# The upper page of an expert's down weights, loaded in two halves, and a down pass that takes all lower rows first

## The chip, the core and the metric

The kernel runs on one of the eight cores of a Trainium2 chip. A core has TensorE (PE) for matmuls, VectorE (DVE) and ScalarE (ACT) for elementwise work and for emptying PSUM, GpSimd (POOL), and SyncE (SP), which here issues nearly all loads. All loads of SP go through one queue (q1), served by the core's 16 DMA engines. The metric is the device time of one execution in microseconds.

## What is computed

One layer on 256 tokens of width 1024: a mixer (chunked attention and spatial gating, merged by gates) and then a mixture of experts, in which each token goes to 4 of 32 experts. The second part is the one that matters here:

```python
h = rmsnorm(x, g_pre_ffn) * (1 + sc2) + sh2
logits = h @ w_router + b_router                 # top 4 of 32 per token, softmax over the four
for e in experts:                                # x_e: the tokens that chose e
    gu = x_e @ w_gate_up[e] + b_gate_up[e]       # 1024 x 2048 f32, 8 MB
    act = min(gu[:, :1024], 7) * sigmoid(1.702 * min(gu[:, :1024], 7)) * (clip(gu[:, 1024:], -7, 7) + 1)
    y_e = act @ w_down[e] + b_down[e]            # 1024 x 1024 f32, 4 MB
out = x + gt2 * rmsnorm(sum of gate * y_e over the chosen experts)
```

All weights are float32. The 32 experts together have 384 MB of them, and each is read once.

## The kernel before

The mixer takes the first part of the span, and its pages of weights pass through a ring of five places. From about 270 us on, the experts run one after the other, each on a list of the tokens that chose it. The list is cut into blocks of 64 tokens, the last of which is narrow (32 tokens) where it is short enough. A 64-token block runs as matmuls of 64 columns of stationary data by 512 moving ones (rows with 128*64), a narrow one as 32 by 256 (rows with 128*32), four to a step k instead of two. There are 37 blocks: 27 experts have one, five have two.

A block on PE is, in order: the gather of its tokens (L1418), the bias (L1427), transposes (L1433), the gate-up pass over k = 0..7 (L1454), `combine` of the block before (L1399), transposes of the activations (L1440) and of the combine table (L1467), and the down pass over eight k (L1483), which ends with `s_y`. The down pass multiplies rows k of `w_down`: k = 0..3 stand in the lower page `dlo_w`, k = 4..7 in the upper page `dhi_w`.

**Where the weights stand.** An expert has six pages of 2 MB: four of gate-up (`gu_w`, two slots, so that experts take turns), the lower down page (`dlo_w`, two slots), and the upper down page `dhi_w`, of which there is one place only (page 10 of the arena). The next expert's upper page can thus be loaded only once the last block of the expert before has finished its down pass.

**What sets the order of the loads.** SP works through a list written out by hand (L443 to L461). In the turn in which expert j is computed it does: wait until the last block's gate-up pass has used the first page (`s_gfree`), load gate-up page 0 of expert j+2; wait for the second page, load page 1; wait until all blocks of expert j are done (`s_y`), load the upper page of expert j+1; and then, behind that wait and without one of their own, the bias, gate-up pages 2 and 3 and the lower page of expert j+2. After the loop it waits for `s_y` of expert 30 and loads the upper page of expert 31, followed by the residual `x1_back` (1 MB) and `gain2` (0.5 MB). The queue thus serves, per expert, gate-up 0 and 1 (j+2), upper page (j+1), gate-up 2, 3 and lower page (j+2).

**What sets the order of the down pass.** `order` sorts the k so that those come first whose activations are turned first (`s_aTev`, `halves[0]`); k in the second half wait for `halves[1]`. In a narrow block (q = 2) that gives 0, 2, 4, 6, 1, 3, 5, 7, in a 64-token block (q = 4) 0, 1, 4, 5, 2, 3, 6, 7. The wait for the upper page (`s_dhi`) stands at k = 4, thus third in both.

## Time and profile before

| | us |
|---|---|
| median of 3 runs | 1217.56 (1217.47 to 1218.21) |
| the profiled execution, its own time | 1217.57 |
| its span, first to last instruction | 1215.3 |
| PE busy in the span | 1037.6 (85%) |
| PE weight loads | 515.7 (42%) |
| DVE busy | 282.4 (23%) |
| ACT busy | 189.9 (16%) |
| POOL busy | 30.8 (3%) |
| moved by DMA | 464.91 MB, mean 383 GB/s |
| mean granted TensorE clock | 0.943 of full |

The profiled execution lies on the median, and 2.3 us of its time lie outside the span. PE is the busiest engine, but its share is an average over stretches with different limits, so the line of GB/s over 40 slices of 30.4 us each must be read beside it.

### The profile page before, as it was taken

The numbers are of one execution on the slowest core, as the hardware profiler recorded it, in microseconds if no ns is written. First come the engines' busy times: TensorE is split into PE (matmuls) and PEld (weight loads), VectorE is DVE, ScalarE is ACT, GpSimd is POOL, SyncE is SP. The second block draws the span as 40 slices with busy tenths as digits, with TensorE's granted clock in tenths as the row PEclk, the third lists the DMA queues.
The fourth block names the chain that finished last, engine by engine and source line by source line (L and its number), as shares of the span: only waits on it lengthen the run. The fifth ranks groups of instructions, "written<-read, shape, count | busy, mean of one in ns | idle before, by whom it ended". The sixth has DMA issues, their size and how long they took to land.

```text
span 1215.3 us, 21516 instructions
## 1 busy us (share of the span) xinstructions
PE 1037.6 (85%) x8327; PEld 515.7 (42%) x8329; DVE 282.4 (23%) x793; ACT 189.9 (16%) x458; POOL 30.8 (3%) x54
## 2 busy tenths in 40 slices
PE   3899999977786999988988898889898989696966
PEld 2756887643343334324433433343334333233333
DVE  5433554152121111211121112111211121111112
ACT  2112443031010111101111111111111111010102
POOL 1000100130000000000000000000000000000000
PEclk9899999987797999989998999899999999898988
DMA  9979650989999969999999999999999999999996
GB/s 357 390 280 331 256 218 12 422 328 387 425 424 425 427 244 424 425 425 406 426 426 424 404 426 427 425 391 427 426 422 402 428 423 426 427 424 425 425 426 266
DMA packets 59948, 464.91 MB, mean 383 GB/s; under 512 B 5380, under 2 KB 7500, under 8 KB 27032
## 3 DMA queue, kind: packets, MB, share of 16 engines
q1 hardware_dynamic: 59184, 462.47, 92.4%
q0 software_dynamic: 336, 1.07, 0.3%
q10 hardware_dynamic: 408, 1.10, 0.2%
q8 instruction: 14, 0.23, 0.1%
q14 instruction: 6, 0.05, 0.0%
HBM read 462.50 MB, written 2.11 MB: 382 GB/s over the span
## 4 chain that ended last, share of the span: by engine, by line
PE 56%; DMA 36%; DVE 3%; issue 3%; ACT 1%; DVEq 0%; SPq 0%; POOL 0%; ACTq 0%
DMA arena<-in_w_down_dram 34%; PE pp L1454 15%; PE pp L1483 15%; PE pp L1245 5%; PE pp L1178 4%; PE pp L1418 2%; PE pp L1258 2%; PE po L1315 2%; PE pp L1188 2%; PE po L1399 2%; DMA arena<-in_w_ada_dram 2%; PE pp L1427 1%; PE pp L1433 1%; DVE h_sb L788 1%; ACT work L702 1%
## 5 line engine op out<-in xcount | busy, mean ns | idle before, releaser
L1454 PE MATMUL pp<-arena,work 128*32 128x256 f32 (+1 forms) x3840 | 374.6, 446 | 20.1 <-ACT work L702 20.1
L1483 PE MATMUL pp<-arena,work 128*32 128x256 f32 (+1 forms) x1920 | 208.7, 485 | 78.8 <-DMA arena<-in_w_down_dram 78.8
L1454 PEld LDWEIGHTS pp<-arena,work 128*32 128x32 f32 (+1 forms) x3840 | 167.5, 117 | 210.9 <-issue 126.7
L1483 PEld LDWEIGHTS pp<-arena,work 128*32 128x32 f32 (+1 forms) x1920 | 81.6, 130 | 187.0 <-DMA arena<-in_w_down_dram 90.6
L1021 DVE TENSOR_SCALAR work<-pp 128x128 f32<-128x128 f32 (+1 forms) x74 | 25.0, 338 | 403.2 <-PE pp L1454 403.2
L705 ACT ACTIVATE work<-work 128x128 f32<-128x128 f32 (+1 forms) x74 | 25.9, 350 | 403.5 <-DVE work L1021 403.5
L1418 PE MATMUL pp<-h_sb,work 128*32 128x256 f32 (+1 forms) x480 | 60.5, 465 | 33.1 <-issue 28.6
L1015 DVE COPY work<-pp 128x256 f32<-128x256 f32 (+1 forms) x37 | 19.4, 525 | 264.1 <-PE pp L1418 264.1
L1399 PE MATMUL po<-work 64*128 64x512 f32 x304 | 75.5, 615 | 1.2 <-ACT work L721 1.2
L1245 PE MATMUL pp<-arena 128*128 128x256 f32 x256 | 59.1, 390 | 0.0
L788 DVE SCALAR_TENSOR_TENSOR h_sb<-arena,small,h_sb 128x1024 f32<-128x1024 f32 x42 | 53.9, 1284 | 7.1 <-DMA arena<-in_w_ada_dram 5.9
L1245 PEld LDWEIGHTS pp<-arena 128*128 128x128 f32 x256 | 49.1, 194 | 8.9 <-issue 2.2
L1418 PEld LDWEIGHTS pp<-h_sb,work 128*32 128x32 f32 (+1 forms) x480 | 21.6, 121 | 71.3 <-issue 64.0
L1399 PEld LDWEIGHTS po<-work 64*128 64x128 f32 x304 | 26.1, 186 | 41.0 <-issue 39.3
L1178 PE MATMUL pp<-arena 128*128 128x256 f32 x192 | 43.3, 387 | 0.0
L1178 PEld LDWEIGHTS pp<-arena 128*128 128x128 f32 x192 | 37.5, 196 | 6.7 <-issue 1.5
L1033 DVE TENSOR_SCALAR work<-iota,rank 128x64 f32 x74 | 15.4, 251 | 96.3 <-issue 91.3
L1037 DVE TENSOR_SCALAR work<-iota,rank,gate_tab 128x64 f32 x148 | 36.2, 308 | 0.0
L719 ACT COPY work<-pp 128x256 f32<-128x256 f32 x23 | 8.6, 372 | 169.0 <-PE pp L1483 169.0
L702 ACT COPY work<-pp 128x256 f32<-128x256 f32 (+1 forms) x37 | 16.8, 453 | 106.3 <-PE pp L1433 106.3
L1427 PE MATMUL pp<-bgu,pick 4*32 4x256 f32 (+1 forms) x480 | 32.2, 470 | 0.0
L1258 PE MATMUL pp<-arena 128*128 128x256 f32 x128 | 28.4, 380 | 0.0
(219 smaller groups left out, 642.0 us busy)
## 6 DMA issues: line engine op xcount, KB each, us to landing
arena<-in_w_gate_up_dram SPq DMA_DIRECT2D x128, 2048.0 KB, 27.4
arena<-in_w_down_dram SPq DMA_DIRECT2D x64, 2048.0 KB, 24.3
arena<-in_w_ada_dram SPq DMA_DIRECT2D x11, 2048.0 KB, 7.7
arena<-in_w_in_dram SPq DMA_DIRECT2D x5, 2048.0 KB, 16.8
arena<-in_w_gate_dram SPq DMA_DIRECT2D x4, 2048.0 KB, 12.7
arena<-in_w_out_dram SPq DMA_DIRECT2D x2, 2048.0 KB, 10.7
arena<-in_w_ada_dram SPq DMA_DIRECT2D x2, 1024.0 KB, 23.4
arena<-in_w_branch_a_dram SPq DMA_DIRECT2D x1, 2048.0 KB, 7.5
```

The costliest lines, as they stand in the source:

```text
L702: a.copy(hgT[:, 0:w], pp[:, TURN, 0:w]).then_inc(s_turned, 1)
L705: a.activation(sig[:, hh, 0:w // 2], glu[:, hh, 0:w // 2], ACT.Sigmoid, scale=ALPHA).then_inc(s_sig, 1)
L788: ins = v.scalar_tensor_tensor(out=acc[:, n % 2, :], in0=page_k(pg, k), scalar=c_act[:, kk:kk + 1], in1=acc[:, n % 2, :], op0=ALU.mult, op ...
L1037: ins = v.tensor_scalar(selg[:, t, c, :], places, rank[:, t, e], gate_tab[:, t, e], ALU.is_equal, ALU.mult)
L1178: mm = t_.matmul(ps[:, i * TOK:(i + 1) * TOK], page_k(pg, k)[:, m * P:(m + 1) * P], hT[:, k, :], start=(k == 0), stop=(k == KD - 1))
L1245: mm = t_.matmul(ps[:, i * TOK:(i + 1) * TOK], page_k(pg, k)[:, m * P:(m + 1) * P], hT[:, k, :], start=(k == 0), stop=(k == KD - 1))
L1258: mm = t_.matmul(branch_bank(m)[:, half * TOK:(half + 1) * TOK], page_k(page_of(name), k)[:, m * P:(m + 1) * P], src[:, k, :], start=(k == 0),
L1399: mm = t_.matmul(po[:, 2 * t + j, :], selgT[j * TB:(j + 1) * TB, t, :], y_sb[j * TB:(j + 1) * TB, :], start=False, stop=last, skip_group_c ...
L1418: mm = t_.matmul(pp[j * m:(j + 1) * m, TOKS, 0:w], sel[:, t, 0:m], h_sb[:, t, j * w:(j + 1) * w], start=(t == 0), stop=(t == TT - 1))
L1427: t_.matmul(pp[j * m:(j + 1) * m, UP[hh], 0:w].rearrange("p (s f) -> p s f", s=2), pick[rows, r, 0:m], bgu[rows, :, cols], start=True, sto ...
L1454: mm = t_.matmul(pp[j * m:(j + 1) * m, UP[hh], 0:w].rearrange("p (s f) -> p s f", s=2), hgT[:, at:at + m], gu_w[slot][:, k, :, r * PAIR:(r ...
L1483: mm = t_.matmul(pp[j * m:(j + 1) * m, UP[0], 0:w], actT[:, at:at + m], wd[:, j * w:(j + 1) * w], start=(n == 0), stop=(n == KD - 1))
```

## The change

The upper page is loaded by two DMAs of 1 MB, one for k = 4 and 5 and one for k = 6 and 7, each with its own semaphore. PE waits for the first at k = 4 and for the second at k = 6. The down pass takes the k in the order 0, 2, 1, 3, 4, 5, 6, 7 in a narrow block and 0 to 7 in a 64-token block, so the wait for the second half of the activations moves from the fifth to the third step. The matmul that ends the sixth step signals `s_dhi_free`, and on this signal SP loads the first half of the next upper page. The second half, and all that stands behind it, still waits for `s_y`.

```diff
-            def load_dhi(e):
-                sp.dma_start(dhi_w.rearrange("p (g r) d -> p g (r d)", r=2), dn_v[e, :, 2:4, :]).then_inc(s_dhi, 16)
+            def load_dhi(e, r):
+                sp.dma_start(dhi_w[:, 2 * r:2 * r + 2, :].rearrange("p k d -> p (k d)"),
+                             dn_v[e, :, 2 + r, :]).then_inc(s_dhi[r], 16)
...
-            load_dhi(0)
+            for r in range(2):
+                load_dhi(0, r)
...
+                    sp.wait_ge(s_dhi_free, total)
+                    load_dhi(last_e, 0)
                     sp.wait_ge(s_y, total)
-                    load_dhi(last_e)
+                    load_dhi(last_e, 1)
...
-            sp.wait_ge(s_y, sp.snap(done, min_val=1, max_val=NEXP * NBLK))
-            load_dhi(sp.snap(dhi_expert, min_val=0, max_val=NEXP - 1))
+            total = sp.snap(done, min_val=1, max_val=NEXP * NBLK)
+            last_e = sp.snap(dhi_expert, min_val=0, max_val=NEXP - 1)
+            sp.wait_ge(s_dhi_free, total)
+            load_dhi(last_e, 0)
+            sp.wait_ge(s_y, total)
+            load_dhi(last_e, 1)
...
-                order = sorted(range(KD), key=lambda k: (k % q >= q // 2, k))
+                order = sorted(range(KD), key=lambda k: (k >= 4, k >= 6, k % q >= q // 2, k))
                 for n, k in enumerate(order):
-                    if k == 4:
-                        pe.wait_ge(s_dhi, dhi_landed)
-                    if n == KD // 2:
+                    if k in (4, 6):
+                        pe.wait_ge(s_dhi[k // 2 - 2], dhi_landed)
+                    if n == 2:
                         pe.wait_ge(s_aTev, halves[1])
...
+                    if n == 5:
+                        mm.then_inc(s_dhi_free, 1)
```

How it moves instructions is seen at two places. First PE's queue in the down pass of a narrow block of the first slot (the matmul is L1483 before and L1492 now; `s_dlo0` is the lower page, `s_dhi` the upper one, `s_aTev` the turned activations). Before:

```order
L1483 MATMUL pp<-arena,work 32x256 [waits s_dlo0]
L1483 MATMUL pp<-arena,work 32x256 x7
L1475 ISA
L1483 MATMUL pp<-arena,work 32x256 [waits s_dhi]
L1483 MATMUL pp<-arena,work 32x256 x7
L1483 MATMUL pp<-arena,work 32x256 [waits s_aTev]
L1483 MATMUL pp<-arena,work 32x256 x11
L1483 MATMUL pp<-arena,work 32x256 [waits s_selTev]
L1483 MATMUL pp<-arena,work 32x256 x3
```

Now:

```order
L1492 MATMUL pp<-arena,work 32x256 [waits s_dlo0]
L1492 MATMUL pp<-arena,work 32x256 x7
L1492 MATMUL pp<-arena,work 32x256 [waits s_aTev]
L1492 MATMUL pp<-arena,work 32x256 x7
L1484 ISA
L1492 MATMUL pp<-arena,work 32x256 [waits s_dhi0]
L1492 MATMUL pp<-arena,work 32x256 x7
L1492 MATMUL pp<-arena,work 32x256 [waits s_dhi1]
L1492 MATMUL pp<-arena,work 32x256 x3
L1492 MATMUL pp<-arena,work 32x256 [waits s_selTev]
L1492 MATMUL pp<-arena,work 32x256 x3
```

Of the 32 matmuls 24 stood behind the wait for the upper page; now 16 stand behind the first half's wait, and 8 of these behind the second half's. (The profile counts each of these f32 matmuls twice, so a narrow down pass is x64 in its rows and one k is x8.)

Second, SP's queue in one turn of the loop (L372 and L373 load gate-up, L402 and L403 the upper page, L398 and L399 the lower page). Before:

```order
L372 DMA arena<-in_w_gate_up_dram 128x4096 [waits s_gfree]
L402 ISA [waits s_y]
L402 DMA arena<-in_w_down_dram 128x2x2048
L454 ISA
L369 DMA bgu<-in_b_gate_up_dram 4x2x256 x2
L372 ISA
L372 DMA arena<-in_w_gate_up_dram 128x4096
```

Now:

```order
L373 DMA arena<-in_w_gate_up_dram 128x4096 [waits s_gfree]
L403 ISA [waits s_dhi_free]
L403 DMA arena<-in_w_down_dram 128x2048
L403 ISA [waits s_y]
L403 DMA arena<-in_w_down_dram 128x2048
L459 ISA
L370 DMA bgu<-in_b_gate_up_dram 4x2x256 x2
L373 ISA
L373 DMA arena<-in_w_gate_up_dram 128x4096
```

One load of half the size has moved ahead of the wait for `s_y`, and everything behind the upper page stands where it stood.

## Rows read from the trace of the kernel before

**Rows 1.** The page's second part: GB/s moved in each of 40 slices.

```profile
GB/s 357 390 280 331 256 218 12 422 328 387 425 424 425 427 244 424 425 425 406 426 426 424 404 426 427 425 391 427 426 422 402 428 423 426 427 424 425 425 426 266
```

**Rows 2.** Waits: engine, line, releaser, us in total, times, longest.

```profile
PE pp L1483 <- DMA arena<-in_w_down_dram: 78.8, 18, 10.2
```

**Rows 3.** Timeline of PE, 1061 to 1126: start, us, engine, line, work, [idle before].

```profile
1061.79 5.35 PE L1483 MATMUL pp<-arena,work 128*32 128x256 f32 x48 [10.19 <-DMA arena<-in_w_down_dram]
...
1091.53 5.37 PE L1483 MATMUL pp<-arena,work 128*64 128x512 f32 x24 [0.64 <-DMA arena<-in_w_down_dram]
...
1121.39 4.86 PE L1483 MATMUL pp<-arena,work 128*32 128x256 f32 x48 [10.13 <-DMA arena<-in_w_down_dram]
```

**Rows 4.** By stretch: PE, PEld, DVE, ACT, POOL busy; granted clock, DMA share, GB/s.

```profile
520.93:640.83 119.90, 106.16 (x975) 45.37 (x975) 21.61 (x75) 14.74 (x41) 0.00 (x0) 0.97 1.00 420
640.83:762.00 121.17, 105.99 (x974) 45.26 (x974) 21.61 (x75) 14.74 (x41) 0.00 (x0) 0.98 1.00 420
762.00:882.15 120.15, 107.04 (x974) 45.49 (x974) 21.60 (x75) 14.75 (x41) 0.00 (x0) 0.97 1.00 417
882.15:1002.18 120.03, 107.75 (x975) 45.35 (x975) 21.59 (x75) 14.74 (x41) 0.00 (x0) 0.97 1.00 419
1002.18:1181.15 178.97, 139.74 (x1104) 56.16 (x1105) 26.72 (x90) 17.77 (x48) 0.00 (x0) 0.90 1.01 425
```

**Rows 5.** Timeline of PE, 288 to 450: first expert's down pass, then the long hole.

```profile
288.36 3.66 PE L1483 MATMUL pp<-arena,work 128*32 128x256 f32 x64
...
390.02 5.32 PE L1483 MATMUL pp<-arena,work 128*32 128x256 f32 x48 [10.17 <-DMA arena<-in_w_down_dram]
...
417.16 1.94 PE L1483 MATMUL pp<-arena,work 128*64 128x512 f32 x8
419.56 5.37 PE L1483 MATMUL pp<-arena,work 128*64 128x512 f32 x24 [0.46 <-DMA arena<-in_w_down_dram]
...
446.19 7.09 PE L1483 MATMUL pp<-arena,work 128*64 128x512 f32 x32
```

**Rows 6.** Timeline of SP, loads only: first turns and the long hole.

```profile
292.23 0.38 SPq L402 DMA_DIRECT2D arena<-in_w_down_dram  x1
...
433.56 3.10 SPq L372 DMA_DIRECT2D arena<-in_w_gate_up_dram  x2
453.47 0.38 SPq L402 DMA_DIRECT2D arena<-in_w_down_dram  x1
```

**Rows 7.** Busy time by stretch at three holes, columns as in rows 4.

```profile
291.00:296.00 5.00, 1.02 (x20) 0.37 (x12) 1.31 (x6) 1.10 (x3) 0.00 (x0) 1.00 0.85 288
...
444.00:458.00 14.00, 13.39 (x114) 5.26 (x114) 3.12 (x11) 2.40 (x6) 0.00 (x0) 1.00 0.33 118
...
692.00:698.00 6.00, 3.96 (x72) 1.81 (x64) 0.94 (x4) 1.47 (x4) 0.00 (x0) 1.00 0.85 318
```

**Rows 8.** Timeline of PE, 670 to 693: a two-block expert.

```profile
670.86 5.37 PE L1483 MATMUL pp<-arena,work 128*64 128x512 f32 x24 [1.29 <-DMA arena<-in_w_down_dram]
...
689.45 3.66 PE L1483 MATMUL pp<-arena,work 128*32 128x256 f32 x64
```

**Rows 9.** Timeline of all engines, 1181 to 1207: the end.

```profile
1181.15 5.35 PE L1483 MATMUL pp<-arena,work 128*32 128x256 f32 x48 [10.00 <-DMA arena<-in_w_down_dram]
...
1186.73 0.38 SPq L402 DMA_DIRECT2D arena<-in_w_down_dram  x1
...
1200.28 3.66 PE L1483 MATMUL pp<-arena,work 128*32 128x256 f32 x64
...
1206.46 0.69 DVE L1083 TENSOR_TENSOR arena<-po,gain 128x512 f32<-128x512 f32 x1 [7.28 <-PE po L1399]
```

**Rows 10.** DMA issues of SP after 1186.5: us from issue to landing last.

```profile
arena<-in_w_down_dram SPq DMA_DIRECT2D x1, 2048.0 KB, 14.2
...
gain<-gain_dram SPq DMA_DIRECT2D x1, 512.0 KB, 17.0
```

**Rows 11.** Busy time by stretch around the last long wait, columns as in rows 4.

```profile
1181.15:1186.50 5.35, 5.35 (x52) 2.33 (x56) 0.00 (x0) 0.00 (x0) 0.00 (x0) 0.50 1.01 432
```

More of the change, by code:

```diff
@@ L278, in block_program @@
         s_dlo = [sem(f"s_dlo{b}") for b in range(2)]
-        s_dhi = sem("s_dhi")
+        s_dhi = [sem(f"s_dhi{r}") for r in range(2)]
+        s_dhi_free = sem("s_dhi_free")
         s_nblk, s_selg = sem("s_nblk"), sem("s_selg")
```

## The prediction

> **What bounds the kernel now.** I read the line of GB/s first [rows 1]. From the eleventh slice on it stands at 422 to 428 nearly everywhere, the highest the kernel reaches: the expert part is bound by the load queue. What deviates is lost time: one slice at 244, a few between 391 and 406, and the last at 266. Then the waits: PE waits 18 times for a down page in the down pass, 78.8 us in all [rows 2]. That looks like the thing to gain, but it is not: while the queue runs at 425, PE's wait is only the other side of a full queue. The timeline shows it. Upper pages land at 1061.79, 1091.53 and 1121.39 [rows 3], and six in a row take 178.97 us, or 29.83 us each, at 425 GB/s [rows 4]. Nothing that PE does sooner makes such a stretch shorter. Time can come only from three places: holes in the queue, the tail behind the last landing, and the cost of a load.
>
> A hole arises since there is one place for the upper page. SP loads it after `s_y`, and all that follows queues behind that wait. Behind a landed upper page some 22 us of other pages are queued. An expert with one block is through in time; one with two is not, and the queue runs dry.
>
> **Prices.** One k of the down pass is 3.66 / 8 = 0.46 us in a narrow block [rows 5], and 5.35 / 6 = 0.89 us after a long wait [rows 3], where the granted clock is 0.50, that is 1.2 GHz [rows 11]. In a 64-token block it is 7.09 / 8 = 0.89 us [rows 5]. Half an upper page is 1.05 MB, 2.47 us at 425 GB/s, so the first half lands 2.5 us before the second. In the long hole the stretch 444 to 458 moved 14 x 118 kB/us = 1.65 MB [rows 7], 3.9 us at full rate, of which about 1.2 stood ahead of the hole; so data flowed again near 455.3, 1.8 us after the issue at 453.47 [rows 6].
>
> **Step 1, the first hole.** The first expert's down pass ends at 292.02 [rows 5], the load follows at 292.23 [rows 6] into a queue that is drying (288 GB/s from 291 to 296 [rows 7]: 5 x 137 / 425 = 1.6 us lost). Its first half will be issued two narrow k earlier, 0.9 us. The half covers 2.5 us, so that the second, issued after `s_y`, follows without a gap. Gain 0.9, and everything in the queue up to the next hole comes 0.9 earlier.
>
> **Step 2, the long hole,** behind the one expert with two 64-token blocks. Its chain starts at the landing at 390.02: six k, 5.32 us, to 395.34 [rows 5]. Now four k are done before the page, two before its second half, and only k = 6 and 7 follow the landing: 1.8 us, 3.6 earlier, 4.5 with step 1. The next block reaches its down pass at 412.7 instead of 417.16 [rows 5], and does four k by 416.3. Its halves land at 419.56 - 0.9 - 2.5 = 416.2 and 418.7; k = 6 and 7 end at 420.4 instead of 424.93. The second block has no wait and ends at 448.8 instead of 453.28; its sixth step at 447.0. The load comes at 447.2 instead of 453.47, 6.3 us earlier. The two gate-up loads of 433.56 [rows 6] move by 4.5 as well, so the small hole in front of them closes. Against it: more matmuls may run at 1.2 GHz, since the block that follows starts 3.6 us sooner after the landing; before, the clock rose at about the end of the down pass (at 1121.39 the 48 matmuls took 4.86 instead of 5.35 [rows 3], so their last part was already fast). The 64-token gather and bias behind it could lose up to 2 us. I take 0.5 and have 5.8 for steps 1 and 2 together, bounds 4.3 and 6.3.
>
> **Step 3, the holes behind the four experts of one 64-token and one narrow block.** Example: the page lands at 670.86; three quarters of a down pass, 5.37 us; the narrow block ends at 693.11 [rows 8]; the hole is seen as 318 GB/s from 692 to 698 [rows 7]. Now `s_dhi_free` comes 1.8 + (693.11 - 676.23) - 0.9 = 17.8 us after the landing, and data 1.8 us later, at 19.6, while the queue lasted 22. So the hole closes with some 2.4 us to spare, which also covers the 2 us that the clock may cost. What the holes are worth, in two ways. By rate: the four stretches run at 420, 420, 417 and 419 instead of 425 [rows 4], which is 1.4 + 1.4 + 2.3 + 1.7 = 6.8 us. By landings: 16 experts took 481.25 us [rows 4], at 29.83 each they would take 477.3, so 4.0. I take the middle, 5.4.
>
> **Step 4, the tail.** The last upper page is issued at 1186.73 [rows 9] and lands 14.2 us later [rows 10], at 1200.9, 19.8 us after the one before (1181.15). The last block comes to its down pass at 1200.28, so it hardly waits, and ends at 1203.94 [rows 9]. Now the block starts 3.6 earlier, is at its down pass at 1196.7 (1198.2 if the clock costs 1.5), is through k = 0 to 5 by about the landing, and ends 0.9 us behind it, at 1201.9 on the old scale: 2.0 earlier. But `gain2`, last in the queue, lands 17.0 us after its issue near 1187.7 [rows 10], at 1204.7, and DVE wants it at 1206.46 - 2.0 = 1204.5 [rows 9]: what comes next is late by 0.2. I take 1.7, bounds 0.5 and 1.8.
>
> **Step 5, what is added.** There are 31 more loads in the loop. In the dense stretch an expert has eight loads (two of them tiny) at 425; if the difference to the best slice (428 [rows 1]) is laid on them, they cost 0.2 us per expert, 0.026 each, 0.8 for 31. I take 0.4, bounds 0 and 0.8. The added wait on PE is for data that was awaited anyway. The wait for the activations' second half moves two k forward; its copy is done before the down pass starts in narrow blocks and two k (1.8 us) remain in 64-token ones: nothing. SP's added wait holds back only the second half's wait, which ends later anyway.
>
> **Sum.** 5.8 + 5.4 + 1.7 - 0.4 = 12.5 us. The profiled execution took 1217.57, 0.01 from the median; 1205.1. With all bounds at their bad ends 4.3 + 4.0 + 0.5 - 0.8 = 8.0, so 1209.6; at their good ends 6.3 + 6.8 + 1.8 = 14.9, so 1202.7.
>
> **Rivals.**
> *The queue pays for each load (ends slower).* Halves may cost the queue something that two-megabyte loads hide. The dearest row is the restart: 1.8 us from issue to data. Shown in full by 31 halves that would be 56 us: 1261. It turns the sign at (12.5 + 2.4) / 31 = 0.48 us per half, and gives no change between 0.33 and 0.48. Against it: loads follow each other at 425 GB/s with the starts hidden [rows 4], and the contiguous piece per partition stays 8 KB. For it: no 1 MB load stands in the dense part. Slower 0.06, no change 0.05.
> The Trainium skill, "DMA: Bandwidth & Descriptors", section "Bandwidth", speaks against the change: it measures 6.15 us for 1 MB (341 GB/s) against 425 GB/s for 16 MB, with a fixed part of about 2.0 us per DMA. By that fixed part the sum would be 62 us dearer, 1267; the trace disagrees for loads that queue, since 2 MB loads run at 425 in rows 4.
>
> *The halves land together,* if the engines work on both at once. Then only the order counts: four k follow each landing instead of six. Steps 1 and 2 give 0.9 + 1.8 + 1.8 = 4.5, step 3 still 4.0, the tail 0.9, less 0.4: 9.0, so 1208.6. Chance 0.08.
>
> *The clock takes it back.* PE has more work at 1.2 GHz behind every long wait; with all bounds bad and 1 us more in the tail, 1210.6. For it: the fall to 0.50 [rows 11] is there. Against it: the queue, not PE, ends the dense stretches. Chance 0.10.
>
> *The small holes stay,* if 417 to 420 has another cause than `s_y`. Without step 3: 1210.5. Chance 0.05.
>
> **How the numbers follow.** My forecast has 0.64 and lies from 1202.7 to 1208; another 0.02 lies below. The range 1201.5 to 1212 holds these and the three mild rivals. A measurement of this kernel tells 0.2%, 2.4 us, from no change. Faster by more: 0.64 + 0.02 + 0.08 + 0.10 + 0.05 = 0.89; within: 0.05; slower: 0.06.
>
> **What would show it.** Slices from the eleventh on at 424 or more, but for one of about 300 where 244 stood; the restart behind the long hole 6 us earlier; two waits in the down passes, the second at most 0.8 us; 29.8 us from landing to landing; the first half 2.5 us ahead. Dense stretches below 423 GB/s would prove the first rival, and small holes left behind the two-block experts the last.

## The result, and the profile after

| | median us | runs | ratio to the kernel before, 95% |
|---|---|---|---|
| before | 1218.16 | 1217.47 to 1218.69 | |
| changed kernel | 1211.37 | 1209.77 to 1215.44 | 0.9948 (0.9928 to 0.9967) |
| predicted | 1205.1 | 1201.5 to 1212.0 | |

The change saves 6.8 us, where 12.5 were forecast. The sign was right and the time lies inside the range, near its upper end, but the gain came out at about half. The runs also differ more among themselves: those of the changed kernel lie within 5.7 us, and within 4.0 when it was run again; those of the kernel before lie within 1.2 here and, in the larger sets of 9 to 15 runs beside the experiments, within 2.1 to 4.7. The profiled execution is the slowest of the five (1215.44, span 1213.2), so it shows what can go wrong better than what mostly happens; the same kernel profiled again (run `again`, below) had a span of 1209.6.

The page of the profiled execution, GB/s in 40 slices of 30.3 us, answering [rows 1]:

```profile
GB/s 358 385 263 333 256 240 11 421 332 362 424 425 426 425 293 422 424 424 425 427 426 423 382 428 426 425 364 424 425 425 424 425 424 425 426 426 425 426 426 279
```

The slice of the long hole rose from 244 to 293. Of the four slices with small holes (406, 404, 391, 402) the first and the last are closed (425, 425), but the two in the middle are worse than before: 382 and 364. The slice of the first hole (the tenth) is worse as well: 362 instead of 387. Waits for down pages in the down pass are down from 78.8 us to 58.7 [rows 2], now in two parts each:

```profile
PE pp L1492 <- DMA arena<-in_w_down_dram: 58.7, 21, 9.5
```

By stretch, cut at landings of the upper page's second half, answering [rows 4] (PE, PEld, DVE, ACT, POOL busy, granted clock, DMA share, GB/s):

```profile
519.20:638.35 119.15, 106.07 (x975) 44.55 (x975) 21.62 (x75) 14.73 (x41) 0.00 (x0) 0.98 1.01 425
638.35:761.41 123.06, 110.79 (x974) 45.63 (x974) 21.62 (x75) 14.73 (x41) 0.00 (x0) 0.93 1.00 415
761.41:883.26 121.85, 110.30 (x974) 45.46 (x974) 21.62 (x75) 14.73 (x41) 0.00 (x0) 0.93 0.98 410
883.26:1001.56 118.30, 107.80 (x975) 44.70 (x975) 21.62 (x75) 14.73 (x41) 0.00 (x0) 0.96 1.01 425
1001.56:1180.79 179.23, 141.89 (x1105) 54.83 (x1105) 26.73 (x90) 17.75 (x48) 0.00 (x0) 0.89 1.01 426
```

The instructions in a four-expert stretch are the same in number as before, but PE is busy 110.8 and 110.3 us in the second and third instead of 106.0 and 107.0, and the granted clock is 0.93 instead of 0.98 and 0.97. PE works longer on the same work. The timeline of PE shows where, behind the wait that ends at 638.35 (start, us, engine, line, work, [idle before]; L1427 is the gather, L1463 the gate-up pass, L1492 the down pass):

```profile
635.81 1.42 PE L1492 MATMUL pp<-arena,work 128*32 128x256 f32 x16 [3.50 <-DMA arena<-in_w_down_dram]
638.35 1.93 PE L1492 MATMUL pp<-arena,work 128*32 128x256 f32 x16 [1.12 <-DMA arena<-in_w_down_dram]
641.20 3.68 PE L1427 MATMUL pp<-h_sb,work 128*64 128x512 f32 x8 [0.92 <-issue]
...
648.53 16.38 PE L1463 MATMUL pp<-arena,work 128*64 128x512 f32 x64 [0.68 <-ACT work L711]
...
668.10 7.09 PE L1492 MATMUL pp<-arena,work 128*64 128x512 f32 x32
```

The two halves are there as described: two k behind the first and two behind the second (x16 in the rows each, which is 8 matmuls), 2.54 us apart. But the block behind them crawls. The gather takes 3.68 us instead of 1.94, the gate-up pass 16.38 instead of 13.95. The same place in the kernel before (L1418 is the gather there, L1483 the down pass):

```profile
640.83 4.51 PE L1483 MATMUL pp<-arena,work 128*32 128x256 f32 x48 [5.19 <-DMA arena<-in_w_down_dram]
646.19 1.94 PE L1418 MATMUL pp<-h_sb,work 128*64 128x512 f32 x8 [0.86 <-issue]
...
667.64 1.94 PE L1483 MATMUL pp<-arena,work 128*64 128x512 f32 x8
```

The granted clock in that stretch of the changed kernel, and in the same block of the kernel before:

```profile
636.40:653.40 17.00, 14.28 (x60) 3.96 (x50) 0.69 (x1) 1.68 (x4) 0.00 (x0) 0.50 1.01 425
```

```profile
646.19:650.50 4.31, 3.63 (x20) 1.31 (x21) 0.69 (x1) 0.93 (x2) 0.00 (x0) 1.00 0.97 411
650.50:664.45 13.95, 13.95 (x66) 4.57 (x66) 0.77 (x3) 0.35 (x1) 0.00 (x0) 1.00 1.01 428
```

Seventeen microseconds at 1.2 GHz. Before, the block from gather to down pass took 667.64 - 646.19 = 21.45 us; now 668.10 - 641.20 = 26.90. It began 5.0 us sooner and came to its down pass 0.5 later. Two things stand out: the clock, and the gap marked "issue", in which PE waits for nothing that the profile shows. That gap is not new at this place (0.86 us before, 0.92 now). What it does is to keep the way from the landing to the gather from shrinking with the work: before, it took 5.36 us for six k (at the landing of 390.02, where the six k filled 5.32 us, just as long), now 2.85 us for two k that take 1.93. So the gather comes 2.5 us sooner after the landing, where the prediction had 3.6. Clock and gap were the two suspects of the experiments, beside the cost of more loads.

### The profile page after: what moved, and what is told of

The parts are those of the page before. It is cut to its first block, busy times and chain, and to the rows that moved or that the text cites. A ratio compares the mean times of both kernels' runs of the same rounds, so it can differ in the third digit from the quotient of the medians.

```text
span 1213.2 us, 21610 instructions
## 1 busy us (share of the span) xinstructions
PE 1047.9 (86%) x8327; PEld 510.1 (42%) x8329; DVE 282.4 (23%) x793; ACT 189.8 (16%) x458; POOL 30.8 (3%) x54
## 3 DMA queue, kind: packets, MB, share of 16 engines
q0 software_dynamic: 336, 1.07, 0.3%
## 4 chain that ended last, share of the span: by engine, by line
PE 64%; DMA 25%; DVE 5%; issue 4%; ACT 2%; DVEq 0%; SPq 0%; POOL 0%; ACTq 0%
PE pp L1463 22%; DMA arena<-in_w_down_dram 21%; PE pp L1492 12%; PE pp L1254 5%; PE pp L1427 4%; PE pp L1187 4%; PE pp L1267 2%; PE po L1324 2%; PE pp L1197 2%; PE pp L1436 2%; DMA arena<-in_w_ada_dram 2%; PE po L1408 2%; DMA gain<-gain_dram 2%; PE pp L1442 1%; ACT work L711 1%
## 5 line engine op out<-in xcount | busy, mean ns | idle before, releaser
L1463 PE MATMUL pp<-arena,work 128*32 128x256 f32 (+1 forms) x3840 | 384.3, 455 | 20.1 <-ACT work L711 20.1
L1463 PEld LDWEIGHTS pp<-arena,work 128*32 128x32 f32 (+1 forms) x3840 | 165.7, 120 | 223.1 <-issue 137.3
L1492 PE MATMUL pp<-arena,work 128*32 128x256 f32 (+1 forms) x1920 | 199.1, 458 | 58.7 <-DMA arena<-in_w_down_dram 58.7
L1492 PEld LDWEIGHTS pp<-arena,work 128*32 128x32 f32 (+1 forms) x1920 | 76.3, 121 | 161.1 <-DMA arena<-in_w_down_dram 73.0
L1427 PE MATMUL pp<-h_sb,work 128*32 128x256 f32 (+1 forms) x480 | 67.7, 504 | 40.4 <-issue 36.0
L1427 PEld LDWEIGHTS pp<-h_sb,work 128*32 128x32 f32 (+1 forms) x480 | 22.3, 128 | 82.6 <-issue 77.2
L1436 PE MATMUL pp<-bgu,pick 4*32 4x256 f32 (+1 forms) x480 | 34.7, 494 | 0.0
```

Of the source, the lines that this page charges most:

```text
L1427: mm = t_.matmul(pp[j * m:(j + 1) * m, TOKS, 0:w], sel[:, t, 0:m], h_sb[:, t, j * w:(j + 1) * w], start=(t == 0), stop=(t == TT - 1))
L1436: t_.matmul(pp[j * m:(j + 1) * m, UP[hh], 0:w].rearrange("p (s f) -> p s f", s=2), pick[rows, r, 0:m], bgu[rows, :, cols], start=True, sto ...
L1463: mm = t_.matmul(pp[j * m:(j + 1) * m, UP[hh], 0:w].rearrange("p (s f) -> p s f", s=2), hgT[:, at:at + m], gu_w[slot][:, k, :, r * PAIR:(r ...
L1492: mm = t_.matmul(pp[j * m:(j + 1) * m, UP[0], 0:w], actT[:, at:at + m], wd[:, j * w:(j + 1) * w], start=(n == 0), stop=(n == KD - 1))
```

## The experiments

All were timed in 5 rounds or more beside the kernel before (1217.6 to 1218.2 in every job). For each profiled execution the table gives the points that the steps of the prediction speak of: the landing of expert 4's upper page, the issue of the load behind the long hole, the landings behind experts 8, 24 and 30 (start of the matmul that waited for the page or its second half; ~ where only the first half was waited for and 2.5 us are added), and the span's end.

| kernel | median | exp. 4 | issue | exp. 8 | exp. 24 | exp. 30 | span |
|---|---|---|---|---|---|---|---|
| before | 1218.2 | 390.0 | 453.5 | 520.9 | 1002.2 | 1181.2 | 1215.3 |
| changed | 1211.4 | 391.9 | 451.4 | 519.2 | 1001.6 | 1180.8 | 1213.2 |
| again | 1212.4 | 390.0 | 449.7 | 517.3 | 997.0 | 1176.4 | 1209.6 |
| order_only | 1213.2 | 390.5 | 452.5 | 520.2 | 998.4 | 1177.4 | 1210.6 |
| split_only | 1213.1 | 392.4 | 453.9 | 521.2 | 999.0 | 1178.3 | 1211.8 |
| late_load | 1212.7 | 390.1 | 451.9 | 519.3 | 998.5 | 1177.8 | 1211.9 |
| fill | 1209.9 | ~391.9 | 449.4 | 518.2 | ~996.6 | ~1175.8 | 1208.1 |
| hoist | 1209.9 | 390.9 | 449.4 | 516.9 | 994.8 | 1174.0 | 1206.4 |

**The changed kernel again.** No edit; it was run beside the next three.

> The changed kernel once more, beside the three others on the same chip. Two theories stand. The clock theory: behind a long wait PE now works in short pieces with gaps between them, stays at 1.2 GHz some 10 us longer than before, and the 64-token block behind the wait takes up to 5.5 us more, so the holes in the load queue come back. The queue theory: the split loads cost the queue time. Both expect 1209 to 1213 us for the median here, with runs further apart than those of the kernel before, since it hangs on where in the clock's decisions a landing falls; the clock theory expects the profile to show stretches of 14 us and more at a granted clock of 0.50 in front of or inside 64-token blocks.

1212.38 (1209.07 to 1213.03), ratio 0.9948 (0.9935 to 0.9962). The same code, the same landing as before at 390.0, and the small holes behaved otherwise than in the first profile: from expert 8 to 24 it took 479.8 us against 482.4 in the first profile and 481.3 in the kernel before. Slow blocks are there as well (behind expert 8 it took 19.6 us from gate-up to down pass instead of 17.1), in another place: which block runs longest at the low clock differs between the two profiles. It is a likely cause of the wider spread, but no run isolates it.

**The order alone.**

```diff
-                order = sorted(range(KD), key=lambda k: (k % q >= q // 2, k))
+                order = sorted(range(KD), key=lambda k: (k >= 4, k >= 6, k % q >= q // 2, k))
...
-                    if n == KD // 2:
+                    if n == 2:
                         pe.wait_ge(s_aTev, halves[1])
```

> The new order of the down pass alone (all lower rows first, wait for the activations' second half at the third step), with one load of the upper page issued after s_y, as before. Behind a landing four k follow instead of six, 3.55 us instead of 5.35 at the low clock. Clock theory: the shorter continuous work, followed by about 1 us in which PE waits for its own sequencer, leaves the clock low into the next block as in the changed kernel; gain at the holes 1 to 2 us each at most and part of it lost again: 1213 to 1217. Queue theory: this kernel has no split loads, so it shows the whole gain of the order: 1208 to 1210 by the sum of the prediction for that case (9 us).

1213.18 (1212.80 to 1213.66), 0.9961 (0.9947 to 0.9974). The 9 us that the expectation took from the prediction's rival "the halves land together" are no fair price, since they hold 2.7 us for the early release, which this kernel lacks, and 0.4 off for the loads. What is left for the order is 6.7 (1.8 in the long hole, 4.0 in the small ones, 0.9 in the tail); 5.0 were gained. The time lies inside the range of the clock theory, at its lower end. But the clock theory, as put in the expectation, is not borne out: the clock came back in time. PE's timeline behind the same wait:

```profile
639.52 3.64 PE L1483 MATMUL pp<-arena,work 128*32 128x256 f32 x32 [5.69 <-DMA arena<-in_w_down_dram]
643.18 2.39 PE L1418 MATMUL pp<-h_sb,work 128*64 128x512 f32 x8
...
```

3.64 us of work without a gap, a gather of 2.39, and five runs within 0.9 us. So a kernel without slow blocks still gains only 5: a second term of the prediction must be too large. From expert 8 to 24 it took 478.2 us, 3.1 less than before. The page still shows dips there (slices of 420, 410, 409 and 409 GB/s, stretches of 421 to 424), yet 16 experts at 29.83 us each would take 477.3: by the landings only 0.9 us was left to gain.

**The halves alone,** both loaded after `s_y`, the old order, waits at k = 4 and k = 6.

```diff
-                    load_dhi(last_e)
+                    load_dhi(last_e, 0)
+                    load_dhi(last_e, 1)
...
-                    if k == 4:
-                        pe.wait_ge(s_dhi, dhi_landed)
+                    if k in (4, 6):
+                        pe.wait_ge(s_dhi[k // 2 - 2], dhi_landed)
```

> The two half loads alone, both issued after s_y, with the old order of the down pass (waits at k = 4, third, and k = 6, fourth). It measures the cost of 32 more loads in the queue. Clock theory: the loads cost nothing that can be seen, five k of continuous work follow the last landing, the time is that of the kernel before within 2 us: 1216 to 1219. Queue theory: the 6 us that are missing are the price of the loads, at 0.2 us each: 1222 to 1225, and landings of upper pages in the dense stretch more than 30.0 us apart instead of 29.83.

1213.08 (1211.85 to 1214.37), 0.9957 (0.9944 to 0.9971). Both theories were wrong: five us are gained by the halves alone. The queue theory falls with it, since 32 more loads made nothing slower. What I had overlooked is the 64-token block, whose old order 0, 1, 4, 5, 2, 3, 6, 7 has the second half's rows last anyway. With two semaphores it gets, without any new order, all that the change could give it, and the narrow blocks get 0.9 us:

```profile
637.94 1.08 PE L1489 MATMUL pp<-arena,work 128*32 128x256 f32 x8 [4.30 <-DMA arena<-in_w_down_dram]
640.51 4.37 PE L1489 MATMUL pp<-arena,work 128*32 128x256 f32 x40 [1.49 <-DMA arena<-in_w_down_dram]
645.03 2.19 PE L1424 MATMUL pp<-h_sb,work 128*64 128x512 f32 x8
```

Expert 8 to 24 took 477.8 us, no more than in any other kernel of the table. So for the small holes it is enough that PE comes through its chain some two microseconds sooner; by the landings more would be worth at most 0.5.

**Without the early release.** The changed kernel with both halves loaded after `s_y`.

```diff
-                    sp.wait_ge(s_dhi_free, total)
-                    load_dhi(last_e, 0)
                     sp.wait_ge(s_y, total)
+                    load_dhi(last_e, 0)
                     load_dhi(last_e, 1)
```

> The changed kernel, but both halves are loaded after s_y; s_dhi_free is gone. It measures what the early release of the first half is worth. The prediction gave it 0.9 us at the first hole and 1.8 at the long one. If that holds, the time is 1.5 to 3 us above the changed kernel: 1213 to 1215. If half a page early is worth nothing, since the second half and what follows still wait for s_y, it is 1211 to 1213, the same as the changed kernel.

1212.65 (1212.08 to 1215.02), 0.9960 (0.9947 to 0.9974): that is in the lower of the two expected ranges. By the medians the early release is worth 0.3 to 1.3 us, less than the runs differ. The traces are clearer at the long hole. With equal landings at 390.0 the load is issued at 449.71 with it (run `again`) and at 451.89 without, and from the issue to the landing behind expert 8 it is 67.6 and 67.4 us: what is issued early arrives early. SP's loads in run `again` and in the kernel without the early release:

```profile
449.71 2.04 SPq L403 DMA_DIRECT2D arena<-in_w_down_dram  x2
```

```profile
451.89 0.85 SPq L402 DMA_DIRECT2D arena<-in_w_down_dram  x2
```

**Filling the gap between the halves.** The lower rows that need the second half of the activations stand between the two waits.

```diff
-                order = sorted(range(KD), key=lambda k: (k >= 4, k >= 6, k % q >= q // 2, k))
+                order = [0, 2, 4, 5, 1, 3, 6, 7] if q == 2 else [0, 1, 4, 5, 2, 3, 6, 7]
...
-                    if n == 2:
+                    if n == (3 if q == 2 else 4):
...
-                    if n == 5:
+                    if k == 5:
                         mm.then_inc(s_dhi_free, 1)
```

> The changed kernel with another order in the down pass: 0, 2, 4, 5, 1, 3, 6, 7 in a narrow block and 0, 1, 4, 5, 2, 3, 6, 7 in a 64-token block. The lower rows 1 and 3 (2 and 3) stand between the two waits for the upper page and fill the 2.5 us between the landings, so that PE works without a gap from the first landing on for 5.3 us, and the first half is released after four steps. Clock theory: the clock rises again by the end of the down pass, the next 64-token block runs at full clock as before, the holes behind the two-block experts close: 1204 to 1208. Queue theory: as the changed kernel, 1209 to 1213.

1209.87 (1207.52 to 1210.40), 0.9925 (0.9912 to 0.9939), on the same chip 2.5 us under the changed kernel (their intervals overlap a little). Not the 1204 to 1208 that I expected, as the holes are worth less. Behind expert 12 the mechanism is as it was put: one wait, 5.29 us of work without a gap, and the block behind it runs like the one before:

```profile
635.30 5.29 PE L1492 MATMUL pp<-arena,work 128*32 128x256 f32 x48 [3.31 <-DMA arena<-in_w_down_dram]
640.66 2.25 PE L1427 MATMUL pp<-h_sb,work 128*64 128x512 f32 x8
...
645.27 13.95 PE L1463 MATMUL pp<-arena,work 128*64 128x512 f32 x64 [0.67 <-ACT work L711]
```

It has a price of its own: the half that is released four steps before `s_y` covers 2.5 us of queue, but `s_y` comes 3.5 us later, and from issue to landing behind expert 8 it takes 68.9 us instead of 67.6.

**Idle matmuls, first try.** Results go to a free PSUM bank that nobody reads.

```diff
+                    if k == 4 and m == NARROW and slot == 0:
+                        with pe.If(late):
+                            for page_, count in ((0, 3), (1, 2)):
+                                pe.wait_ge(s_gup[1][page_], landed)
+                                for _ in range(count):
+                                    t_.matmul(pp[:, UP[1], :], ident[:], h_sb[:, 0, 0:512], start=True, stop=True,
+                                              skip_group_check=True)
+                    if k == 6 and m == NARROW and slot == 0:
+                        with pe.If(late):
+                            t_.matmul(pp[:, UP[1], :], ident[:], h_sb[:, 0, 0:512], start=True, stop=True,
+                                      skip_group_check=True)
```

> The changed kernel with idle matmuls in narrow blocks of the first slot from the fifth expert on: three of 128x512 once gate-up page 0 of the next expert has landed, two once page 1 has, one between the two waits for the upper page. Their results go to a free PSUM bank and are not read. They keep PE busy during the long waits and change nothing in the loads. Clock theory: the clock does not fall or is back at the landing, the 64-token blocks behind the waits run as in the kernel before (gather to gate-up 4.3 us, gate-up to down pass 17.1), the holes close: 1206 to 1209, and less spread than 1209 to 1215. If the clock is not the cause, the idle matmuls (some 5 us in blocks that do not wait) bring nothing or cost time: 1211 to 1216.

1229.98 (1228.22 to 1233.40), 1.0103: slower, against the expectation. The blocks behind long waits do run at full clock (behind expert 4: gather to gate-up 4.3 us, gate-up to down pass 17.1), but a narrow block that has nothing to wait for pays for each idle matmul, and such blocks stand on PE's chain to the next hole. The slices of the four small holes fall to 349, 339, 341 and 313 GB/s. One such block:

```profile
587.71 1.93 PE L1503 MATMUL pp<-arena,work 128*32 128x256 f32 x32
589.58 4.56 PE L1488 MATMUL pp<-h_sb,ident 128*128 128x512 f32 x10
594.07 1.07 PE L1503 MATMUL pp<-arena,work 128*32 128x256 f32 x16
```

**Idle matmuls only where a long wait is,** that is, if the next expert has two blocks: one after each of the two landings, one between the halves.

```diff
+                next_nb = pe.value_load(nblk_i[0:1, bass.ds(i * 2 + 1, 1)], min_val=1, max_val=NBLK)
...
+                    if k == 4 and m == NARROW and slot == 0:
+                        with pe.If(next_nb >= 2):
+                            for page_ in range(2):
+                                pe.wait_ge(s_gup[1][page_], landed)
+                                t_.matmul(pp[:, UP[1], :], ident[:], h_sb[:, 0, 0:512], start=True, stop=True,
+                                          skip_group_check=True)
```

> The changed kernel with idle matmuls only where the long wait in front of a two-block expert is: one of 128x512 after the landing of gate-up page 0 of the next expert, one after page 1, one between the two waits for the upper page, if the next expert has two blocks. PE needs one more register load per turn for it. The first such kernel proved the clock and lost the time with idle matmuls in blocks that do not wait; this one puts none there. Clock theory: the 64-token blocks of the four experts with one wide and one narrow block run gather to gate-up in 4.3 us and gate-up to down pass in 17.1, no hole of more than 1.6 us lost remains behind them, and the time is 1209.5 to 1211 with less spread than the changed kernel's. If the clock costs nothing that reaches the end, 1211 to 1213 as before.

1210.12 (1208.12 to 1210.98), 0.9933 (0.9920 to 0.9946), as the clock theory expected, though the interval still overlaps that of the changed kernel (0.9935 to 0.9962 in `again`). The traces are clearer. Behind expert 12, where the changed kernel crawled:

```profile
633.92 1.07 PE L1502 MATMUL pp<-arena,work 128*32 128x256 f32 x16
...
638.77 1.94 PE L1427 MATMUL pp<-h_sb,work 128*64 128x512 f32 x8 [1.68 <-issue]
...
643.08 13.95 PE L1463 MATMUL pp<-arena,work 128*64 128x512 f32 x64 [0.68 <-ACT work L711]
```

The loads and their order are those of the changed kernel; PE was kept at work (and reads one register more per turn), and the 64-token block takes 21.45 us from gather to down pass, 5.5 us less. All five blocks behind such waits, from expert 4 to expert 20, take 21.4 us. The dense stretch, where this kernel has no idle matmuls, is the control within the same run: there one 64-token block again took 19.9 us from gate-up to down pass.

**Register loads ahead of the turn.** It tests the 0.9 us "issue".

```diff
...
             with pe.Fori(0, NEXP // 2) as i:
+                sizes = [(pe.value_load(nblk_i[0:1, bass.ds(i * 2 + slot, 1)], min_val=1, max_val=NBLK),
+                          pe.value_load(wide_i[0:1, bass.ds(i * 2 + slot, 1)], min_val=0, max_val=NBLK))
+                         for slot in range(2)]
                 for slot in range(2):
-                    nb = pe.value_load(nblk_i[0:1, bass.ds(i * 2 + slot, 1)], min_val=1, max_val=NBLK)
-                    wide = pe.value_load(wide_i[0:1, bass.ds(i * 2 + slot, 1)], min_val=0, max_val=NBLK)
+                    nb, wide = sizes[slot]
```

> The changed kernel, but PE reads the table entries of both experts of a turn (four register loads) ahead of the first expert's blocks instead of each expert's two between the blocks. It tests the second suspect: 2.83 us pass between the last landing and the next gather where the two k take 1.93 at the low clock, since PE's sequencer, held at the wait, has the register loads still before it. Sequencer theory: the time from the last landing to the next gather falls to 2.0 to 2.2 us behind even experts, PE has no gap of 0.9 us there, and the time is 1208 to 1211. If the gap is something else, it stays at 2.8 and the time at 1209 to 1213.

1209.88 (1208.68 to 1211.32), 0.9937 (0.9924 to 0.9951). From the last landing to the next gather behind expert 4, first the changed kernel, then this one:

```profile
391.94 1.93 PE L1492 MATMUL pp<-arena,work 128*32 128x256 f32 x16 [0.61 <-DMA arena<-in_w_down_dram]
394.77 1.97 PE L1427 MATMUL pp<-h_sb,work 128*64 128x512 f32 x4 [0.89 <-issue]
```

```profile
390.95 1.93 PE L1492 MATMUL pp<-arena,work 128*32 128x256 f32 x16 [0.58 <-DMA arena<-in_w_down_dram]
392.81 2.98 PE L1427 MATMUL pp<-h_sb,work 128*64 128x512 f32 x8
```

2.83 us against 1.86, and the gap is gone: it was the two register loads that PE reaches only behind the wait. (That its sequencer is held at the wait together with the engine is the explanation that fits; the rows show only that the gap goes with the loads.) The loads are not free where they stand now: from expert 8 on, PE has a gap of 2.1 to 3.1 us at the start of a turn, where it had 1.6 at most before. Up to expert 24 a gap of 1.3 us within the turn is gone for it, and in the dense stretch a wait of 5 us and more follows, which takes it up:

```profile
1029.26 1.34 PE L1427 MATMUL pp<-h_sb,work 128*32 128x256 f32 x13 [2.41 <-issue]
```

The clock still cost something where PE met the landing at 1.2 GHz (gather to gate-up 5.35 us behind expert 4, 5.50 behind expert 8). Behind experts 12, 16 and 20 PE had waited only 1.4 us for the second half, its two k ran at full clock (1.07 us), and gather to gate-up took 4.4.

**Together, and the best version.** `fill_hoist` has both edits:

> The order 0, 2, 4, 5, 1, 3, 6, 7 (narrow) and 0, 1, 4, 5, 2, 3, 6, 7 (64 tokens) together with the early register loads. Both theories (clock, sequencer) expect the best time so far, as their terms add: the order gave 1209.9, the loads are worth up to 0.9 us at the long hole and as much in the tail: 1207.5 to 1209.5.

1210.12 (1208.77 to 1210.54), 0.9932 (0.9919 to 0.9946): they do not add up; the likely reason is that each alone already closes the small holes. `hoist_warm` is the early register loads with the few idle matmuls, run twice:

> The same idle matmuls in the kernel with the early register loads. The holes behind the 64-and-narrow experts are closed there already (1209.9), so what is left for the clock is the chain in front of the long hole. Both terms together: clock 0 to 1 us less, 1208.5 to 1210. It is also the candidate for the best version of this study.

1208.85 (1208.35 to 1210.55), 0.9930 (0.9917 to 0.9943).

> The kernel with early register loads and idle matmuls in front of two-block experts once more (1208.85 before). If it stands apart from the one without the idle matmuls (1209.9), the median is again under 1209.5; if not, it is 1209.5 to 1210.5.

1209.71 (1208.13 to 1211.29), 0.9933 (0.9920 to 0.9947). It does not stand apart. Five kernels (`fill`, `hoist`, `fill_hoist`, `warm_few`, `hoist_warm`) end at 1209 to 1210, 0.7% under the kernel before. All lie under the changed one (1211.4 and 1212.4), but the intervals of the ratios touch or overlap. `fill` is the simplest of them. `order_hoist`, one load and the new order with early register loads, shows that the halves are needed for it:

> The new order with one load of the upper page after s_y, as in the second experiment (1213.2), and the early register loads. What remains of the difference to the same kernel with halves (1209.9) is the worth of the halves themselves. Sequencer theory: four k behind the landing take 3.6 us at the low clock, longer than the sequencer's 2.8, so the early loads bring little here: 1212 to 1213.5, and the halves are worth 2 to 3.5 us. If it falls to 1210, the halves are worth nothing beside the sequencer.

1214.24 (1213.06 to 1215.45), 0.9972 (0.9962 to 0.9982): no better than without the early loads, as the sequencer theory says for four k behind a landing, though 0.7 us above the range that it was given. Beside the early loads the halves are worth some 4 us.

**What a load costs.** The first try split each gate-up page of the kernel before by partitions.

```diff
...
+                for rows in (slice(0, 64), slice(64, P)):
+                    sp.dma_start(gu_w[slot][rows, 2 * i:2 * i + 2, :, :].rearrange("p k s f -> p (k s f)"),
+                                 gu_v[e, rows, i, :]).then_inc(s_gup[slot][i], 16)
```

> The kernel before with each gate-up page of the expert part loaded by two DMAs of 1 MB, one per half of the partitions, back to back, so that pieces stay 16 KB and nothing else moves: 128 more loads. It measures the price of a load by itself. In the kernels with halves the dense stretch took 29.87 to 29.90 us per expert against 29.83, which would be 0.04 to 0.07 us per extra load: 5 to 9 us here, 1223 to 1227, and 30.0 to 30.1 us per expert. If a queued load costs nothing, 1217 to 1219 and 29.83.

2047.74 us (2007.59 to 2179.73; the trace is of an execution of 2127.71). A packet of 16 KB takes 1240 ns at the median instead of 614, and one of 8 KB, though most of these belong to down pages over all partitions, 598 instead of 312. So the loads of 64 partitions slow the whole queue, and the run says nothing on the number of loads. Two further kernels separate number and shape, `split_lower` with the lower page in two loads of the shape that the change uses, `double_cols` with the gate-up pages in two loads over all partitions:

```diff
+                for r in range(2):
+                    sp.dma_start(dlo_w[slot][:, 2 * r:2 * r + 2, :].rearrange("p k d -> p (k d)"),
+                                 dn_v[e, :, r, :]).then_inc(s_dlo[slot], 16)
```

> The kernel before with the lower down page loaded by two DMAs of 1 MB, back to back, in the shape that the change uses for the upper page (8 KB per partition, all partitions), and nothing else: 32 more loads that wait for nothing and release nothing. If a queued load costs what the prediction took as its upper bound, 0.026 us, the time is 1217.5 to 1219; if it cost 0.2 us, as it would have to for the missing 6 us, 1223 to 1225 and 30.0 us per expert in the dense stretch.

```diff
+                for r in range(2):
+                    sp.dma_start(gu_w[slot][:, 2 * i + r, :, :].rearrange("p s f -> p (s f)"),
+                                 gu_v[e, :, i, 2048 * r:2048 * r + 2048]).then_inc(s_gup[slot][i], 16)
```

> The kernel before with each gate-up page loaded by two DMAs of 1 MB over all 128 partitions, 8 KB per partition instead of 16: 128 more loads. The last experiment split the same pages by partitions and took 2048 us. If the number of loads did that, this one takes about as long; if it was the 64 partitions per load, this one runs at over 400 GB/s: 1218 to 1235, slower than before by the smaller pieces and 128 times the price of a load.

`split_lower`: 1217.63 against 1217.96, ratio 0.9998 (0.9989 to 1.0007). One of its eleven executions took 1941.49 us, which nothing here explains; the other ten lie from 1216.90 to 1219.70. `double_cols`: 1225.56 (1223.61 to 1226.62), 1.0058 (1.0045 to 1.0072). The stretch from 1010 to 1150 of `double_loads`, `double_cols` and `split_lower`, GB/s last:

```profile
1010.00:1150.00 140.00, 89.60 (x736) 35.70 (x738) 13.52 (x47) 10.49 (x29) 0.00 (x0) 0.80 0.94 204
```

```profile
1010.00:1150.00 140.00, 111.57 (x842) 43.78 (x836) 18.53 (x61) 13.52 (x36) 0.00 (x0) 0.91 1.01 421
```

```profile
1010.00:1150.00 140.00, 112.11 (x834) 44.11 (x826) 21.21 (x69) 14.29 (x38) 0.00 (x0) 0.93 1.01 425
```

32 more loads of 1 MB in a full queue cost nothing that can be measured: by the interval between 1.3 us less and 0.9 us more. The Trainium skill, "DMA: Bandwidth & Descriptors", section "Anatomy of one DMA — SWDGE (gpsimd) path", puts a fixed part of about 2.0 us on each DMA that GpSimd issues. For 32 loads that would be an estimated 64 us; these loads, which SP issues into a full queue, show none of it. Of the 7.6 us of `double_cols`, 128 more loads could then take 3.6 at most (four times 0.9); at least some 4 us belong to the pieces of 8 KB instead of 16. Two packets of 8 KB take 624 ns at the median, one of 16 KB 614. That is argued from `split_lower` and the packets, not shown by a kernel of its own.

## Why the prediction was half right

**What bounds the kernel:** right. The queue runs at 424 to 426 GB/s between holes in every kernel, and the gain came from holes and tail only.

**Step 1, the first hole, 0.9 us:** the early release worked, the gain did not arrive. From the start of the first down pass to the load it took 3.87 us before and 3.00 now (289.21 to 292.21), the 0.9 that was forecast. But the landing of expert 4 came at 390.0 to 392.4 in the kernels of the table, in the kernel before at 390.0, and the changed kernel alone had 391.9 and 390.0. When PE starts the experts it runs at 1.2 GHz for a while, and the first gate-up pass took 8.64 us before and 9.74 and 9.40 in the changed kernel's two profiles. That delays the first down pass, and the loads behind it, by about as much as the step gains. The pass took 8.6 to 9.7 us in five kernels with one load of the upper page and 9.0 to 10.1 in all that load it in halves; whether the change itself lengthens it stays open.

**Step 2, the long hole, 5.8 with step 1:** the mechanism was right, the term mis-sized. From the landing at expert 4 to the issue behind the hole it took 63.5 us before and was to take 58.1 without, 58.6 with the 0.5 us for the clock. It took 59.5 and 59.7. The step that failed is "only k = 6 and 7 follow the landing: 1.8 us": from the landing to the gather it is 2.83 us, and the missing 1.0 is the gap at PE's register loads, shown by `hoist` (58.5). The clock took 1.0 there (gather to gate-up 5.6 us instead of 4.6) instead of 0.5. With step 1 gone as well, the issue came 3.8 us earlier in `again`, and 2.0 in the first profile.

**Step 3, the small holes, 5.4:** the largest miss, in two parts. *What they are worth:* of the two estimates the landings gave 4.0, the rates 6.8, and I took the middle. `order_only`, `split_only`, `fill` and `hoist` took 477.8 to 478.3 us from expert 8 to expert 24 against 481.3 before: 3.0 to 3.4 us, some 0.8 for each of the four holes, where the term had 1.35. A fall of GB/s over a few us was read as lost time, though the end is set by landings: `order_only` keeps dips of 409 to 420 GB/s and loses 0.9 us by the landings. *Whether they close:* "which also covers the 2 us that the clock may cost" failed. The clock took 5.5 and 5.0 us of PE's time in two blocks of the first profile (26.90 and 26.79 us from gather to down pass instead of 21.45 and 21.80). There the queue lost more than before in this stretch (482.4 us); in `again` 1.5 us were gained. The low clock was a rival with a chance of 0.10, but priced at no more than 2 us per block, since I took the time at 1.2 GHz from the kernel before, where PE works through 5 us without a gap behind each wait. The change itself takes that away: work of 1.9 us, a gap, 1.9 us, a gap. The forecast that the second wait is at most 0.8 us failed with it: it is 0.5 to 0.6 where the two k between the halves take 1.9 us, and up to 1.7 where they run at full clock. The rival that the small holes have another cause than `s_y` falls: in `hoist` three of the four stretches run at 425 and 426 GB/s.

**Step 4, the tail, 1.7:** right in the first profile, where from expert 30's landing to the end it took 32.4 us instead of 34.1. The last block there (the last landing, the gather, the down pass; then DVE's first use of `gain2`):

```profile
1180.79 1.90 PE L1492 MATMUL pp<-arena,work 128*32 128x256 f32 x16 [0.54 <-DMA arena<-in_w_down_dram]
1183.50 1.07 PE L1427 MATMUL pp<-h_sb,work 128*32 128x256 f32 x16 [0.81 <-issue]
...
1197.98 3.76 PE L1492 MATMUL pp<-arena,work 128*32 128x256 f32 x64
```

```profile
1204.36 0.69 DVE L1092 TENSOR_TENSOR arena<-po,gain 128x512 f32<-128x512 f32 x1 [7.46 <-DMA gain<-gain_dram]
```

DVE now waits for `gain2` and no longer for PE, the wait that was forecast to be next. In `again` the low clock fell into the last `combine` (3.40 us instead of 1.99), DVE waited for PE after all, and only 1.0 us was left.

**Step 5, the loads, 0.4:** not contradicted, and not resolved: `split_lower` allows up to 0.9 us for 32 loads. The dense stretch took 179.2 to 179.4 us in the kernels of the table with halves, and 179.0, 179.1 and 179.4 in `before`, `order_only` and `order_hoist` without them. The rival that would have made the kernel slower falls, since it needed 0.48 us for each load.

**The sum,** with `again`, whose time is near the median: 3.6 at expert 8 (5.8 forecast), 1.5 from there to expert 24 (5.4), -0.4 in the dense stretch (-0.4 for all loads), 1.0 in the tail (1.7): 5.7 of 12.5. That the first median lies inside the range is partly luck: the second, 1212.38, lies just outside. The chance of 0.64 for 1202.7 to 1208 was too high: it treated the clock as a small correction to each step, when it decided step 3.

## What to carry to other kernels

When an engine's work behind a wait is cut short or into pieces, look at what the long piece used to cover: here, in the long hole, the six steps behind the page hid PE's register loads, and at all such waits they brought its clock back up; both costs came out when only two were left. Put the independent work between two waits rather than in front of them. And price a hole in a queue by the distance of landings, not by the depth of the dip in GB/s.

## What the runs showed that I had not expected

- The clock stayed at 1.2 GHz for 17.0 us (636.4 to 653.4) though PE was busy for 14.28 of them. In the kernel before, the stay behind the same wait ended within the 4.5 us of uninterrupted work behind the landing. A 64-token block then takes up to 26.9 us to its down pass instead of 21.45, so these matmuls are not indifferent to the clock.
- Loads to 64 of the 128 partitions halve the rate of the whole queue: 204 GB/s against 421 (1010 to 1150 us) for the same pages in as many loads over all partitions, and 2048 us against 1226.
- A gap on PE can come from register loads behind a wait: it went away when they were moved ahead of it, and 2.83 us from landing to gather became 1.86.
